# A two-layer hybrid decoder trunk on one core: memory norm weights folded into the weight split, and an earlier split of up-projection groups

## The reference, cut to what matters

```python
def reference(x, mem, positions, ...):
    h = x
    for l in range(DEPTH):
        y = hybrid_mixer(rms_norm(h, mix_norm_pre[l]), positions, w_in[l], ..., w_out[l])
        h = h + rms_norm(y, mix_norm_post[l])
        y = memory_cross_attention(rms_norm(h, x_norm_pre[l]), rms_norm(mem, mem_norm[l]),
                                   x_wq[l], x_wk[l], x_wv[l], x_wo[l])
        h = h + rms_norm(y, x_norm_post[l])
        y = conv_ffn(rms_norm(h, ffn_norm_pre[l]), ffn_w_up[l], ffn_conv_w[l], ffn_conv_b[l], ffn_w_down[l])
        h = h + rms_norm(y, ffn_norm_post[l])
    return h

def memory_cross_attention(h, mem_n, wq, wk, wv, wo):      # 4 heads x 256
    q, k, v = h @ wq, mem_n @ wk, mem_n @ wv               # split in heads
    p = softmax(einsum('bshc,bmhc->bhsm', q, k) * 256 ** -0.5)
    return einsum('bhsm,bmhc->bshc', p, v) @ wo
```

## Time and profile before

| | us |
|---|---|
| median of 3 runs | 860.92 (859.11 to 861.6) |
| the profiled execution | 860.67 |
| its span | 858.7 |
| TensorE busy in the span | 824.8 |
| VectorE busy | 615.4 |
| ScalarE busy | 499.3 |

### The profile page before, as it was taken

One profiled execution on the slowest core, in us unless ns is written; L12 is line 12 of the kernel. 1 busy time (PEld: TensorE's weight loads), 2 busy tenths in 40 slices (PEclk: granted clock), 3 DMA queues, 4 the chain that ended last, 5 costly groups with the idle time before them and its releaser, 6 DMA issues.

```text
span 858.7 us, 12984 instructions
## 1 busy us (share of the span) xinstructions
PE 824.8 (96%) x5152; PEld 737.0 (86%) x5152; DVE 615.4 (72%) x1080; ACT 499.3 (58%) x765; POOL 28.4 (3%) x53
## 2 busy tenths in 40 slices
PE   3999999999999799999999999999999979999997
PEld 2898898888889799998899889887988879999885
DVE  5689996674665778877577999847558477778653
ACT  4555876565646665564454578655646456665541
POOL 1000000010000000000020000001001000000000
PEclk9999999999999899999999999999999989999999
DMA  9656344573463455557647553447445435655661
GB/s 342 213 172 177 119 147 128 158 245 108 141 227 118 152 181 173 186 177 239 188 150 254 166 167 105 145 146 232 159 142 168 139 97 192 195 181 174 214 194 49
DMA packets 40363, 147.31 MB, mean 172 GB/s; under 512 B 4528, under 2 KB 4656, under 8 KB 40304
## 3 DMA queue, kind: packets, MB, share of 16 engines
q1 hardware_dynamic: 38144, 138.90, 50.7%
q0 software_dynamic: 2160, 7.59, 2.7%
HBM read 145.43 MB, written 1.05 MB: 171 GB/s over the span
## 4 chain that ended last, share of the span: by engine, by line
PE 78%; DVE 12%; ACT 4%; issue 2%; DMA 2%; POOL 1%; SPq 0%; DVEq 0%; POOLq 0%; ACTq 0%
PE acc L1359 7%; PE acc L1360 7%; PE acc L1361 7%; DVE wlo L817 4%; PE acc L1399 3%; PE acc L1401 3%; PE acc L1342 3%; PE acc L1400 3%; PE acc L1343 3%; PE acc L1344 3%; DVE arena L1090 3%; PE psAB L1343 2%; PE psAB L1342 2%; PE psAB L1344 2%; PE psCD L1310 2%; PE psAB L1361 2%
## 5 line engine op out<-in xcount | busy, mean ns | idle before, releaser
L817 DVE TENSOR_TENSOR wlo<-raw,whi 128x1024 fp32r<-128x1024 f32 x240 | 287.7, 1221 | 97.8 <-ACT whi L478 96.1
L478 ACT ACTIVATE whi<-raw 128x1024 fp32r<-128x1024 f32 x240 | 249.4, 1057 | 94.6 <-PE acc L1344 45.3
L1359 PE MATMUL acc<-xT_hi,whi 128*128 128x256 f32 x448 | 130.5, 291 | 9.2 <-DVE wlo L817 9.2
L1360 PE MATMUL acc<-xT_lo,whi 128*128 128x256 f32 x448 | 128.8, 287 | 0.0
L1361 PE MATMUL acc<-xT_hi,wlo 128*128 128x256 f32 x448 | 128.6, 287 | 0.0
L1359 PEld LDWEIGHTS acc<-xT_hi,whi 128*128 128x128 f32 x448 | 88.1, 197 | 12.5 <-DVE wlo L817 9.6
L1360 PEld LDWEIGHTS acc<-xT_lo,whi 128*128 128x128 f32 x448 | 88.1, 197 | 0.2
L1361 PEld LDWEIGHTS acc<-xT_hi,wlo 128*128 128x128 f32 x448 | 88.0, 196 | 0.0
L1359 PE MATMUL psCD<-xT_hi,whi 128*128 128x256 f32 x192 | 54.6, 285 | 0.0
L1361 PE MATMUL psCD<-xT_hi,wlo 128*128 128x256 f32 x192 | 54.3, 283 | 0.0
L1360 PE MATMUL psCD<-xT_lo,whi 128*128 128x256 f32 x192 | 54.3, 283 | 0.0
(11 more groups left out here) (268 smaller groups left out, 2015.0 us busy)
## 6 DMA issues: line engine op xcount, KB each, us to landing
raw<-stream_dram SPq DMA_DIRECT2D x256, 512.0 KB, 4.1
gpre<-gain_dram POOLq DMA_DIRECT2D x7, 512.0 KB, 5.4
gpost<-gain_dram POOLq DMA_DIRECT2D x6, 512.0 KB, 5.1
memn<-mem_dram SPq DMA_DIRECT2D x2, 512.0 KB, 6.1
h<-x_dram SPq DMA_DIRECT2D x1, 1024.0 KB, 12.3
out_dram<-h SPq DMA_DIRECT2D x2, 512.0 KB, 2.7
cst<-const_dram SPq DMA_DIRECT2D x1, 896.0 KB, 16.6
gpre<-gain_dram SPq DMA_DIRECT2D x1, 512.0 KB, 5.5
```

The lines of the kernel that those rows point to most:

```text
L478: act.activation(home(g)[0], raw[:, s * GW:(s + 1) * GW], ACT.Copy).then_inc(w_hi.sem, 1)
L817: dve.tensor_tensor(lo, raw[:, cols], hi.bitcast(F32), ALU.subtract).then_inc(w_lo.sem, 1)
L1359: pe.matmul(dst, whi[:, cols], hi[:, toks], start=k == 0 and c % 2 == 0, stop=False)
L1360: pe.matmul(dst, whi[:, cols], lo[:, toks], start=False, stop=False)
```

## The change

Four things change together.

1. The memory is transposed and split as it comes, once, for both layers. Its norm weights multiply the rows of the weights instead: for the 16 key and value groups of a layer, each split is two operations of 512 columns per engine, with a per-partition scalar `gain_of(l, k)`. The weights' 2 x 8 rows are loaded small and transposed by TensorE once. The roots multiply the values in their copy (`v_rows`) and the scores in the maximum (`cross_max`, where a multiply-and-max against `rs_wide` writes the scaled scores to `xp`, which the exponential reads); `rs_wide`, the roots along the columns, comes out of one small product. The value half G_WV0 now opens the layer, and the key half G_WK0 stands where it was.
2. The start is ordered anew: the first memory tile and four weight groups ahead of x; 18 matmuls on a zero tile (`wait_busy`) while TensorE has nothing else; the first value product in the order in which its operands come; the trig arguments behind the first splits, and the constants, the convolution's parameters and gpost later.
3. The last query group of cross attention finishes half its output first (`last_queries`), so that the scores of head 2 can begin after it.
4. Up groups 8 to 14 are split further ahead.

```diff
+def memory_chunk(g):
+    for g0 in (G_WV0, G_WK1, G_WK0, G_WV1):
+        if g0 <= g < g0 + PER_TILE:
+            return (g - g0) * UNITS
+    return None
...
         def _(sp_):
             sp_.dma_start(cst[:, 0:CC_TRI], consts[:, 0:CC_TRI]).then_inc(head_in.sem, 16)
+            for l in range(DEPTH):
+                sp_.dma_start(gain_rows[l * KC:(l + 1) * KC, :],
+                              gains[l, MEM_G, :].rearrange("(c p) -> c p", p=P)).then_inc(mgain_in.sem, 16)
             sp_.dma_start(memn[:, 0:D], mem[0:P, :]).then_inc(mem0_in.sem, 16)
-            sp_.dma_start(gpre[:, :], gains[0, MEM_G, :].partition_broadcast(P)).then_inc(mgain_in.sem, 16)
...
+            for g in range(RING):
+                group(g)
             sp_.dma_start(memn[:, D:2 * D], mem[P:2 * P, :]).then_inc(mem1_in.sem, 16)
...
+            for t in range(TOK):
+                sp_.dma_start(h[:, t * D:(t + 1) * D], x[t * P:(t + 1) * P, :]).then_inc(x_in[t].sem, 16)
...
             def split_group(l, g):
...
-                act.activation(home(g)[0], raw[:, s * GW:(s + 1) * GW], ACT.Copy).then_inc(w_hi.sem, 1)
+                k = memory_chunk(g % GROUPS)
+                if k is None:
+                    e = act.activation(home(g)[0], raw[:, s * GW:(s + 1) * GW], ACT.Copy)
+                else:
+                    for u in range(UNITS):
+                        e = act.activation(home(g)[0][:, u * NT:(u + 1) * NT],
+                                           raw[:, s * GW + u * NT:s * GW + (u + 1) * NT], ACT.Copy, scale=gain_of(l + g // GROUPS, k + u))
+                e.then_inc(w_hi.sem, 1)
...
                 input_hi(0, 0)
                 split(6)
-                transposed_in(KT[:, 0:4 * SEQ], psAB, G_WK0 + PER_TILE, KT_in)
                 split(G_DLQ + PER_TILE - 1)
...
                 split(G_CV + PER_TILE - 1 + AHEAD)
+                act.wait_ge(mem_rs.sem, TOK)
+                v_rows(0, psAB, G_WV0 + PER_TILE)
...
                 turn_to_up()
+                split(G_UP + 2 * HELD + 2)
                 rows_out(1, rows[0], G_UP + HELD)
-                split(G_UP + 2 * HELD + 1)
+                split(G_UP + 2 * HELD + 3)
                 rows_out(0, rows[1], G_UP + 2 * HELD)
-                split(G_UP + 2 * HELD + 3)
...
             def split_group(l, g):
...
-                dve.tensor_tensor(lo, raw[:, cols], hi.bitcast(F32), ALU.subtract).then_inc(w_lo.sem, 1)
+                k = memory_chunk(g % GROUPS)
+                if k is None:
+                    e = dve.tensor_tensor(lo, raw[:, cols], hi.bitcast(F32), ALU.subtract)
+                else:
+                    for u in range(UNITS):
+                        part_u = slice(u * NT, (u + 1) * NT)
+                        e = dve.scalar_tensor_tensor(lo[:, part_u], raw[:, s * GW + u * NT:s * GW + (u + 1) * NT],
+                                                     gain_of(l + g // GROUPS, k + u), hi[:, part_u].bitcast(F32),
+                                                     ALU.mult, ALU.subtract)
+                e.then_inc(w_lo.sem, 1)
...
                     if i == 0:
-                        split(g_end + 4)
+                        split(g_end + 5)
                     norm_scale(l, i + 1, 1, n_gain)
...
                 def cross_max(hd):
...
-                    own.link(dve.tensor_reduce(st(S_XMX + 2 * b, 2),
-                                               psAB[b][:, :].rearrange("p (t n) -> p t n", t=TOK), AX_X, ALU.max))
+                    own.link(dve.memset(st(S_XMX + 2 * b, 2), -3e38))
+                    for t in range(TOK):
+                        e = dve.tensor_tensor_reduce(xp[:, b, t, :], psAB[b][:, t * SEQ:(t + 1) * SEQ], rs_wide, 1.0,
+                                                     -3e38, ALU.mult, ALU.max, st(S_XMX + 2 * b + t))
+                    own.link(e)
...
-                if not ends(l, 2):
-                    split(G_DOWN + 6 + AHEAD)
-                    dve.wait_ge(gpre_in.sem, gpre_in.at(l, 3))
-                    memory_gain()
...
+            def wait_busy(n):
+                for i in range(n):
+                    pe.matmul(accs[1][0][:, :], idle[:, 0:P], idle[:, :], start=True, stop=True)
...
+                if not l:
+                    pe.wait_ge(diag_set.sem, 1)
+                    pe.matmul(psCD[1][:, 0:SEQ], ones_sq, rs_diag, start=True, stop=True).then_inc(wide_done.sem, 1)
...
-                transposed_product(G_XQ + PER_TILE + 3, 1, X, acc[1], k0=6)
+                last_queries(G_XQ + PER_TILE + 3)
                 x_flip(0)
-                pe.wait_ge(qT_in.sem, qT_in.at(l, TOK + 2))
+                pe.wait_ge(qT_in.sem, qT_in.at(l, TOK + 1))
```

More of the change, by code:

```diff
@@ L264, in hybrid_trunk @@
         cst_in = signal("cst_in", 0, before=1, unit=16)
-        x_in = signal("x_in", 0, before=1, unit=16)
+        x_in = [signal(f"x{t}_in", 0, before=1, unit=16) for t in range(TOK)]
         pos_in = signal("pos_in", 0, before=1, unit=16)
@@ L850, in _ @@
-            for t in range(TOK):
-                cols = slice(2 * t * HALF, (2 * t + 1) * HALF)
-                e = dve.tensor_scalar(ang[:, cols], ang[:, cols], float(np.pi / 2), None, ALU.add)
-            own.link(e)
-            pi = 3.1415925
-            dve.tensor_scalar(trig[:, :], ang, pi, -pi, ALU.min, ALU.max).then_inc(trig_arg.sem, 1)
-            dve.wait_ge(mgain_in.sem, 16)
-            for t in range(TOK):
-                rows = slice(t * D, (t + 1) * D)
-                dve.wait_ge(mem_rs.sem, mem_rs.at(0, t - TOK + 1))
-                dve.scalar_tensor_tensor(xn[:, rows], memn[:, rows], st(S_HRS + t), gpre[:, :],
-                                         ALU.mult, ALU.mult).then_inc(mg_done.sem, 1)
-                if not t:
-                    dve.wait_ge(mem_sq.sem, mem_sq.at(0, 0))
-                    mean_square(S_HMS + 1, S_HSQ + 1).then_inc(mem_ms.sem, 1)
```

394 lines of the change are left out of this document (246 added, 148 removed).

## The result

The changed kernel takes 849.38 us (median; 848.51 to 850.91), the kernel before 861.05 beside it. The ratio is 0.9869, with a 95% interval from 0.9851 to 0.9887: 11.7 us less, where 19.6 were forecast, and 0.4 us beyond the slow end of the range. The profiled execution has a span of 848.5 us against 858.7. The page (busy us and share of each engine; granted clock in 40 slices) answers to the earlier trace rows: TensorE is busy for 98% now, and one dip of the clock is left, in the second slice.

A forecast was written before the change was run, and what follows sets the result against it. TensorE, busy 96%, was taken as the bound, with its waits and half-clock stretches as what could go. Gains 7.8 + 12.2 + 1.7 less costs 1.2, 0.6 and 0.3 made 19.6 us: 841.3, range 836.5 to 849.

The forecast's parts named there:

- the start: Up to the convolution's product on x: it begins at 38.1 instead of 45.9 us, gain 7.8, bounds 5.9 and 9.3.
- the scaled split: Memory key and value groups: two 512-column operations, 0.18 us more each on VectorE; 0.6 at layer 1's turn, elsewhere about 0.
- Up groups: Up stretch: earlier splits remove the 4.6 us wait and slow clock, new wait 1.0 on group 15; gain 12.2 in both layers.
- Transposes in down: Between layers: 16 transposes go from the down product, 1.7 us less of TensorE's own work.
- the first rival: Start: the clock falls while TensorE idles before G_DLQ; 1.9 us of gain go, up to 4 with late data; chance 0.2.
- the turn to layer 1: Turn into layer 1: four value groups add 4 x 0.18 us to VectorE, a value product is 0.15 shorter; cost 0.6.
- the turn to cross attention: Same four groups, but a plain split fills VectorE's 0.5 us wait for the root: 0, from 0.5 worse to 0.3 better.
- the sixteen groups: Key and value groups in the stick-breaking stretch: splits 0.18 us longer each, 2 us or more ahead of use; cost 0, at most 0.5.
- The slower rival: Scaled VectorE splits taking 1.22 us, not 0.75, in each layer's two turns: slower than before, 862 or more; chance 0.02.
- Fewer, larger operations: The skill's overheads would make each scaled split cost 0.06, not 0.18 us more on VectorE, the layer turn 0.3, not 0.6; rows kept.
- Sigmoid: Mixer: V's scaled copy ahead of the sigmoid's table load makes the sigmoid 0.6 us later; cost 0.6 a layer, 1.2 in all.
- Wide product: One 128x256 f32 product for the roots: cost 0.3 us.

The follow-up runs named there:

- plain splits: The changed kernel with the norm weights left out of the memory groups' split, one Copy and one subtraction of 1024 columns each: 842.25 us, ratio 0.9796.
- the copies early: The changed kernel with V's two scaled copies on ScalarE ahead of the last split of the convolution's product: 848.08 us, ratio 0.9857.

## Why the prediction was right and wrong

The forecast of 841.3 was 8 us too low. Two steps failed: the start, 7.8 us forecast and 2.7 found, and the scaled split, of which everything behind the start was put at 0.6 us and cost 5.6.

- **Up groups (12.2):** right. 6.03 and 6.12 a layer, the new wait on group 15 0.76 for 1.0, the clock untouched. Durations from rows, chained by hand, held to 0.3 us over 25 us.
- **Transposes in down (1.7):** right, 1.79.
- **Start (7.8):** a step that failed. The gain was 2.7 in the profile, and about 4.1 where the clock is down for 3.4 us. By the forecast G_DLQ's first split was there at 25.4 and the convolution's product began 12.7 behind it, at 38.1; measured were 28.38 and 14.83. Three terms were missing or small. The table load was not in the chain: 1.28, shown. The transposes, put at 6.9 because the idle matmuls were given 0.43 each "a little less if the clock rises", came at 7.75: the idle matmuls began at 1.46, behind the zeroing of their tile, and eight of them took 3.38 us. Some 1.0 us more was lost in small waits between there and the memory's last mT_lo, which ended at 19.5 and not at 16.4; from it to the split of G_DLQ the forecast was 9.0 and the trace has 8.8. And TensorE fell to 1.2 GHz in the pause, 2.2 us: this is the first rival, priced at 1.9 and given a chance of 0.2; it came in ten of the eleven traces with that pause, and cost the start 0.6 to 0.9 us in nine of them and 2.2 in one. It should have had most of the chance, since my chain itself had a pause of 3.2 us and the trace of before a fall within 2.8.
- **Scaled split (0.6 in the turn to layer 1, 0 in the other turn and the mixer):** the other step that failed; the direction was right, the size was not. VectorE's 0.18 a group was measured as 0.19. ScalarE's was taken at nothing, and is 0.28. The turn to layer 1 costs 1.06 against plain splits. "0, from 0.5 worse to 0.3 better" for the turn to cross attention: against plain splits it is 1.05 a layer, most of which the rest of the change gave back there (net the lead fell by 0.2 from 139 us to the up turn). "Lie ahead of their use by 2 us or more: 0" for the sixteen groups: 1.06 and 1.09 in the stick-breaking stretch of the two layers. The steps there lie at instructions that wait for VectorE's other work (L1185 in the wait shown), which is queued behind the splits, and not for a split. The slower rival named this mechanism, but asked for VectorE operations of 1.22 us; they took 0.75, as the rows had it, and what cost was ScalarE's side as much as VectorE's (1.8 and 2.3 us behind the start), and the two together.
- **Fewer, larger operations.** The Trainium skill, Perfetto Trace Analysis, section Optimizing Scalar/DVE Operations, advises fewer and larger operations. The runs do not speak against it: one plain instruction more for each group costs 1.0 us on ScalarE and 1.5 on VectorE, within the noise, and the 6.3 us of the whole scaled split hold the scale as well. Its 93 ns of access overhead on ScalarE is close to what the second plain copy costs here (2 x 521 against 948, 94 ns), and its 60 ns on VectorE to what a second plain subtraction costs (69). That I set against it the 0.18 of a row was right, but for a reason I did not have: on ScalarE the scalar from a tile costs as much again for each instruction, and on VectorE the scaled operation 61 ns. (The 0.3 that the prediction gives for the turn by that figure is also a slip: 4 x 0.06 less 0.15 are 0.1.)
- **Sigmoid (0.6 a layer):** mechanism right. 0.9 and 0.6 in rope; with the copies early both are gone.
- **Key products.** A term left out: two key groups take 5.9 us where two value groups took 5.6, so the stretch at 121 to 139 costs 0.6 a layer. I had seen the difference, and used it only in the turn, and too small: two value groups take 5.44 us there and two key groups took 5.75, 0.3 less and not 0.15, so that the turn to layer 1 gives the 0.6 back. Read from traces, not tested.
- **Wide product (0.3):** 0.44.

The start missed 5.1 us in the profile, the mixers 1.7 and 1.75, the turns 0.7: 9.25 of the 9.4 us between 19.6 forecast and the 10.2 of the spans. What stays open is what decides how long the clock stays down behind one and the same pause, and whether it falls behind the shorter wait of 2 us ahead of it.

## What to carry to other kernels

Price an added operand, not only an added instruction: a factor folded into a pass "for free" was paid on two engines for each of 32 groups, and it cost as much as all it saved. Slack is shared: two delays that are each covered may together not be, so a chain should be run with all costs on it, and "ready 2 us ahead" checked for what is queued behind as well. In a start, list what each engine must have loaded (tables too) before its first instruction, and fill a pause that you know of.

## What the runs showed of the hardware

- A scale read from a tile costs ScalarE 93 ns per instruction of 512 columns (614 ns against 521 from start to start; 712 against 621 in duration). On VectorE the scaled subtraction takes 61 ns more than the plain one (663 against 602; 746 against 685).
- ScalarE's first table load came behind the wait of a first activation that has two waits (8.43), and ahead of a sigmoid's with one (54.64, with the product ending at 54.89). An activation on one column at the start moves it to 0.74.
- Behind the same pause of 2.67 us the granted clock was at 0.50 for 6.8, 3.4 or 0 us, in single executions of eleven kernels. The changed kernel's own four runs differ too, with a mean clock of 0.995 three times and 0.998 once. In the six kernels with idle matmuls in the pause it stayed at 1.00 there.
- Behind the 2 us wait for the first whi it was at 0.50 for 3.4 us in four traces (in two of the six just named, from 11.3 and 11.7 us on) and stayed at 1.00 in three others with the same wait.
- VectorE instructions of 0.42 and 0.48 us took 1.55 and 1.51 while GpSimd subtracted 512 columns (1.28 and 2.10 us).
